# The head of an eight-core hybrid decoder step: x tiles 0 to 2 at once, v's weights in two halves, the other x tiles behind the first half

## The reference

```python
h = rmsnorm(x, g_mix)
proj = h @ w_in
a = proj[..., :512]
z = gelu(proj[..., 512:1536])          # u | v
u, v = z[..., :512], rmsnorm(z[..., 512:], g_v)
w = where(tril(ones(128, 128)), w_s, 0)
s = einsum('gij,bnjgc->bnigc', w, v in chunks of 128 rows) + b_s
pa = (trailing means of a over 2, 4, 8, 16 rows - a) @ w_pool * s_pool
merged = sigmoid(..) * (pa @ w_pool_out) + sigmoid(..) * ((u * s) @ w_gmlp_out)
x = x + merged @ w_out                 # then a SwiGLU FFN and a last rmsnorm
```

## Time and the profile before

| what | us |
|---|---|
| median of 3 runs | 832.25 |
| the profiled execution, its own time | 831.42 |
| span of its slowest core (core 2) | 829.6 |
| spans of the eight cores | 826.4 to 829.6 |
| PE busy on core 2 | 805.8 (97%) |
| DVE, ACT, POOL busy on core 2 | 380.8, 225.0, 96.2 |

### The profile page before, as it was taken

How to read it: one execution, slowest core, us unless ns; L and a number is a source line. 1 busy time by engine, 2 the same in 40 slices (tenths; PEclk the granted TensorE clock), 3 DMA queues, 4 the chain that set the end, 5 groups by cost and what they waited for, 6 DMA issues and landing times.

```text
span 829.6 us, 12893 instructions; the slowest of 8 cores (826.4 to 829.6 us)
## 1 busy us (share of the span) xinstructions
PE 805.8 (97%) x4423; PEld 425.6 (51%) x4474; DVE 380.8 (46%) x618; ACT 225.0 (27%) x458; POOL 96.2 (12%) x154
## 2 busy tenths in 40 slices
PE   5999999999999999999999999999999999999996
PEld 3465666645666666644444444444444444444442
DVE  3776444468222222265776935446711111115357
ACT  2654322224211211120136352322321111110023
POOL 2720000012000000000312000011200000000001
PEclk9999999999999999999999999999999999999998
DMA  7894155684974543354977417688576444336313
GB/s 167 182 181 84 26 77 77 102 122 86 198 114 69 80 74 66 63 92 65 144 238 112 77 28 135 112 170 136 95 117 102 77 77 77 66 62 102 51 48 155
DMA packets 57315, 85.14 MB, mean 103 GB/s; under 512 B 23373, under 2 KB 23749, under 8 KB 57236
## 3 DMA queue, kind: packets, MB, share of 16 engines
q0 software_dynamic: 30352, 57.97, 45.3%
q1 hardware_dynamic: 26755, 26.09, 11.3%
q10 hardware_dynamic: 146, 0.27, 0.1%
HBM read 128.72 MB, written 9.01 MB: 166 GB/s over the span
## 4 chain that ended last, share of the span: by engine, by line
PE 84%; DVE 6%; issue 3%; DMA 2%; POOL 2%; ACT 2%; DVEq 0%; SPq 0%; POOLq 0%; ACTq 0%
PE ps L347 81%; DMA xbuf<-xp 2%; POOL rs L384 1%; DVE xbuf L367 1%; ACT junk L375 1%; ACT junk L992 1%; DVE xbuf L984 1%; PE ps L746 1%; PE ps L742 1%; DVE ybuf L1017 1%; DVE hb L404 0%; POOL rs L1003 0%; PE ps L695 0%; DVE shr L627 0%; DVE xbuf L874 0%
## 5 line engine op out<-in xcount | busy, mean ns | idle before, releaser
L347 PE MATMUL ps<-hT,ring 128*128 128x384 bf16 (+2 forms) x2698 | 484.1, 337 | 1.2
L347 PEld LDWEIGHTS ps<-hT,ring 128*128 128x128 bf16 x2720 | 265.5, 98 | 206.3
L347 PE MATMUL ps<-ring,ovl 128*128 128x512 bf16 x939 | 207.3, 379 | 1.1
L846 DVE TENSOR_TENSOR ovl<-ftmp,ps 128x384 bf16<-128x384 f32 (+2 forms) x110 | 64.2, 584 | 233.8 <-PE ps L347 226.5
L347 PEld LDWEIGHTS ps<-ring,ovl 128*128 128x128 bf16 x960 | 93.5, 98 | 113.8 <-issue 2.2
L844 ACT ACTIVATE ftmp<-ps 128x384 f32<-128x384 f32 (+2 forms) x110 | 56.3, 515 | 232.0 <-PE ps L347 232.0
L267 POOL DMA_DIRECT2D ring<-wpk x60 | 45.0, 750 | 493.8 <-PE ps L347 459.9
L944 DVE TENSOR_TENSOR xbuf<-xbuf,ps 128x512 f32<-128x512 f32 x64 | 43.4, 687 | 41.2 <-PE ps L347 41.1
L347 PE MATMUL ps<-ovl,ring 128*128 128x384 bf16 (+2 forms) x317 | 62.0, 337 | 0.2
L812 DVE TENSOR_TENSOR shr<-shr,ps 128x384 f32<-128x384 f32 (+2 forms) x40 | 23.4, 585 | 83.3 <-PE ps L347 74.5
L992 ACT ACTIVATE junk<-xbuf 128x512 bf16<-128x512 f32 (+1 forms) x34 | 21.3, 627 | 124.0 <-DVE xbuf L984 120.9
(11 more groups left out here) (90 smaller groups left out, 346.8 us busy)
## 6 DMA issues: line engine op xcount, KB each, us to landing
ring<-wpk POOLq DMA_DIRECT2D x48, 1024.0 KB, 11.2
xbuf<-xp SPq DMA_DIRECT2D x16, 512.0 KB, 6.6
yp<-ybuf SPq DMA_DIRECT2D x11, 512.0 KB, 3.4
ring<-wpk POOLq DMA_DIRECT2D x8, 512.0 KB, 13.0
ring<-wpk POOLq DMA_DIRECT2D x4, 768.0 KB, 8.1
yp<-shr SPq DMA_DIRECT2D x4, 512.0 KB, 2.6
AB<-xp SPq DMA_DIRECT2D x2, 512.0 KB, 6.9
shr<-xp SPq DMA_DIRECT2D x2, 512.0 KB, 11.6
```

Of the source, the lines that this page charges most:

```text
L347: ins = e.matmul(out=out, lhsT=lhs_fn(i), rhs=rhs_fn(i), start=(i == 0), stop=(i == n - 1))
L846: P.op('dve', lambda e: e.tensor_tensor(out=actT[:, f, c0:c0 + W], in0=ftmp[:, fi, :W], in1=PS[bU][:, :W], op=ALU.mult), reads=[('ftmp', f ...
```

## The change

- SP issues x tiles 0, 8, 1 and 2 without a wait. Tiles 3 to 7 wait for the first half of v's weights.
- POOL issues v's weights (block 0) as two transfers of 128 x 2048, each with a semaphore of its own, and only once x tile 0 has landed.
- Blocks 0 and 1 are laid out in pieces of 2048 and 4096 elements a partition instead of 1024 (in both passes).
- v's 8 matmuls of a tile are issued as two parts of 4, one for each half of the weights; v runs one step of the stagger later. Gelu goes to `vg`, a float32 buffer with a place for each tile (it lies where `mergedT` will be), so nothing waits for `ftmp`. The squares of v and its 1/rms come later and in three batches of three tiles, one POOL pair for each batch, and `v_out` after each batch.
- The copies of `gv_rep` and `wb0` on DVE come later (at `i_ == 3`); blocks 1 and 2 are issued at `i_ == 7` and `i_ == 9` and the constants at `i_ == 8`.
- `ws_prep` comes after g = 2 instead of g = 0.

```diff
-WPIECE = 1024
+WPIECE = [2048 if i < 1 else 4096 if i < 2 else 1024 for i in range(len(WBLOCKS))]
...
+        def ring_issue_halves(j, after=()):
+            slot = j % NSLOT
+            off, ne = blocks[j]
+            for h_ in range(2):
+                dst = ring[:, slot, h_ * (ne // 2):(h_ + 1) * (ne // 2)]
+                src = wpk[0:1, off + h_ * 64 * ne:off + (h_ + 1) * 64 * ne].rearrange("o (p e) -> (o p) e", p=128)
+                P.dma('pool',
+                      (lambda e, dst=dst, src=src: e.dma_start(out=dst, in_=src)),
+                      'wh%d' % h_, reads=list(after), writes=[('ring', slot, h_)])
             rstate['issued'] = j + 1
...
-        for slot in range(2, 8):
-            xload(0, slot, after=[('x', 1, 0)])
+        xload(0, 2)
         cdma('pool', ident_b[:, :], c_ident[:, :], 'ident_b', own='c_idb')
-        ring_issue(0)
+        ring_issue_halves(0, after=[('x', 0, 0)])
+        for slot in range(3, 8):
+            xload(0, slot, after=[('ring', 0, 0)])
...
+                def v_mm(t_):
+                    if t_ == 0:
+                        v_part(0, 0)
+                    elif t_ == 1:
+                        v_part(1, 0)
+                        v_part(0, 1)
+                    elif t_ == 2:
+                        v_part(1, 1)
+                        v_part(2, 0)
+                        v_part(2, 1)
+                    else:
+                        v_part(t_, 0)
+                        v_part(t_, 1)
...
+                vsq_at = {9: (0, 1), 10: (2, 3), 11: (4, 5), 12: (6,), 13: (7,), 14: (8,)}
+                vrs_at = {11: 0, 12: 3, 14: 6}
                 warm(10)
-                for i_ in range(n_ + 8):
-                    at(i_ - 3, do_v)
+                for i_ in range(n_ + 6):
+                    at(i_ - 4, v_mm)
                     at(i_ - 1, lambda t_: hst[t_][2]())
                     at(i_ - 1, lambda t_: hst[t_][3]())
                     if i_ == 1:
                         warm(12)
+                    if i_ == 3:
+                        while row_later:
+                            row_later.pop(0)()
                     at(i_ - 2, lambda t_: hst[t_][4]())
-                    at(i_ - 7, lambda t_: vst[t_][2]())
                     at(i_, lambda t_: hst[t_][0]())
                     at(i_, lambda t_: hst[t_][1]())
-                    at(i_ - 6, lambda t_: vst[t_][0]())
-                    at(i_ - 6, lambda t_: vst[t_][1]())
-                    if i_ == 5:
+                    at(i_ - 5, v_gelu)
+                    for t_ in vsq_at.get(i_, ()):
+                        v_sq(t_)
+                    if i_ == 7:
+                        ring_issue(1)
+                    if i_ == 8:
                         late_pool_consts()
                         mid_sp_consts()
-                    if i_ == 8:
+                    if i_ == 9:
                         ring_issue(2)
+                    if i_ in vrs_at:
+                        lo_ = vrs_at[i_]
+                        v_rs(lo_, lo_ + 3)
+                        for t_ in range(lo_, lo_ + 3):
+                            v_out(t_)
...
-                if s == 0 and g == 0:
+                if s == 0 and g == 2:
                     ws_prep()
```

More of the change, by code:

```diff
@@ L549, in build_nc @@
                 hst = [norm_stages(slot, R, col0, gmix_rep, 'gmix', copy_eng='dve') for (slot, R, col0) in hts]
-                vst = {}
                 n_ = len(hts)
+                kv = [newcol() for _ in range(n_)]
                 def at(t_, fn_):
@@ L555, in at, with v_dst, v_part, fn @@
                         fn_(t_)
-                def do_v(t_):
-                    vst[t_] = c_tile(*hts[t_], split=True)
+                def v_dst(t_):
+                    slot, R, col0 = hts[t_]
+                    return vg[:, slot, :] if slot < 8 else ftmp[:R, 0, :]
+                vbank = {}
+                def v_part(t_, h_, wv=wv):
+                    slot, R, col0 = hts[t_]
+                    if h_ == 0:
+                        vbank[t_] = bank()
+                        held.add(vbank[t_])
+                    b = vbank[t_]
+                    def fn(e, wv=wv):
+                        ins = None
+                        for i in range(4 * h_, 4 * h_ + 4):
+                            ins = e.matmul(out=PS[b][:R, :], lhsT=hT[:, i, col0:col0 + R], rhs=wv[:, i, :],
+                                           start=(i == 0), stop=(i == 7))
+                        return ins
+                    P.op('pe', fn, reads=[cres_[h_]] + hT_res([slot]), writes=[('ps', b)])
@@ new lines, in v_mm, with v_gelu @@
+                def v_mm(t_):
[11 more added lines that the diff above has]
+                        v_part(t_, 1)
+                def v_gelu(t_):
+                    slot, R, col0 = hts[t_]
+                    b = vbank[t_]
+                    vd = v_dst(t_)
+                    P.op('act', lambda e: e.activation(out=vd, in_=PS[b][:R, :], func=AF.Gelu_apprx_tanh),
+                         writes=[('vg', slot), ('ps', b)] + ([('ftmp', 0)] if slot == 8 else []))
+                    held.discard(b)
@@ new lines, in v_sq, with v_rs @@
+                def v_sq(t_):
+                    slot, R, col0 = hts[t_]
+                    vd = v_dst(t_)
+                    k = kv[t_]
+                    ji = nxt('jk', 2)
+                    P.op('act', lambda e: e.activation(out=junk[:R, ji, 0:512], in_=vd, func=AF.Square,
+                                                       accum_out=ss[:R, k:k + 1]),
+                         reads=[('vg', slot)], writes=[('ss', k), ('junk', ji)])
+                def v_rs(lo, hi):
+                    ka, kb = kv[lo], kv[hi - 1] + 1
+                    P.op('pool', lambda e: e.tensor_scalar(out=ms[:, ka:kb], in0=ss[:, ka:kb], scalar1=1.0 / 512,
+                                                           scalar2=EPS, op0=ALU.mult, op1=ALU.add),
+                         reads=[('ss', k_) for k_ in range(ka, kb)], writes=[('ms', k_) for k_ in range(ka, kb)])
+                    P.op('pool', lambda e: e.tensor_tensor(out=rs[:, ka:kb], in0=ms[:, ka:kb],
+                                                           in1=mhalf[:, 0:1].to_broadcast([128, kb - ka]), op=ALU.pow),
+                         reads=[('ms', k_) for k_ in range(ka, kb)] + ['mhalf'],
+                         writes=[('rs', k_) for k_ in range(ka, kb)])
@@ new lines, in v_out @@
+                def v_out(t_):
+                    slot, R, col0 = hts[t_]
+                    vd = v_dst(t_)
+                    k = kv[t_]
+                    dst, dres = (vtok[:, slot, :], ('vtok', slot)) if slot < 8 else (vout[:, :], 'vout')
+                    P.op('dve', lambda e: e.scalar_tensor_tensor(
+                        out=dst, in0=vd, scalar=rs[:R, k:k + 1], in1=gv_rep[:R, :], op0=ALU.mult, op1=ALU.mult),
+                         reads=[('vg', slot), ('rs', k), 'gv'], writes=[dres] + ([('ftmp', 0)] if slot == 8 else []))
+                    if slot == 8:
+                        P.op('dve', lambda e: e.tensor_copy(out=vtok[:R, 8, :], in_=vout[:, :]),
+                             reads=['vout'], writes=[('vtok', 8)])
+                        P.dma('sp', lambda e: e.dma_start(out=nvs[:, :], in_=vout[:, :]), 'omisc', reads=['vout'])
@@ L823, in build_nc @@
                             out=mergedT[:, d, c0:c0 + W], in0=gab[:, gi, 0, :W], in1=gab[:, gi, 1, :W], op=ALU.add),
-                             reads=[('gab', gi, 0), ('gab', gi, 1)], writes=[('mergedT', d, c0)])
+                             reads=[('gab', gi, 0), ('gab', gi, 1)],
+                             writes=[('mergedT', d, c0)] + ([('vg', t_) for t_ in range(9)] if s == 0 else []))
                         if s > 0 and carry['late']:
```

32 lines of the change are left out of this document (19 added, 13 removed).

## The result

The changed kernel takes **838.7 us** (median of 4 runs, 836.77 to 838.96) beside 832.06 for the kernel before on the same chip: ratio 1.008, interval 1.0067 to 1.0093. It is slower by 0.8%, where 826.5 was forecast and 829.8 was the end of the range. The profiled execution took 836.77 us. Medians are of all executions; ratios, and what is said of compared runs, leave out those of the chip's slower state, in which the cores of a die ran much longer at a lower clock.

The account below looks back on a forecast made before the run. Start of projection a (A), set on core 2 by x's arrival, was taken to bound the kernel. Terms -4.15 (A) and -1.5 (after v) made -5.65 us: 831.42 to 825.8, median 826.6, stated 826.5; range 823.5 to 829.8.

Parts of the forecast that it names:

- block 1: Weight block needed at A: lands at 36.2, 1.6 us ahead; later block 2 and constants also cost nothing.
- A: Start of projection a on PE: forecast 37.85, 4.15 us less than 42.0, moving the end by as much.
- rival 2: Block 1 takes 14 us, lands at 40.2 and becomes the wait at A: 828.8 us, chance 0.10.
- rival 5: Slower: tiles 3 to 7 hang on a slow first half of v's weights, 834.2 us, chance 0.03.
- Block 1's issue: On POOL behind tile 6's 1/rms: tile lands near 23.8, 1/rms 2.37 us later, so issue at 26.2.
- H: Time the first half of v's weights has landed: taken as 12.5, bounds 10.6 and 14.
- from H to the landing of tile 3: Gated x load in the head: 4.9 us plus some 0.7 for the second half, 5.6 in all.
- from there to its transpose: Tile 3's landing to the end of `hb` in the head: 3.65 us, transpose beginning at 21.75.
- from there to A: PE work behind tile 3's transpose: 5 transposes and 7.5 tiles of v, 15.2 us, plus 0.9 for clock.
- The low clock: PE's slower matmuls after idling 2 to 3 us in the head: 0.9 us, bounds 0 and 1.75.
- the batches: After v, the trailing sums begin earlier against PE, removing waits: 1.5 us off, bounds 0 and 1.8.
- whatever the head did: The rest of the program from A to the end has the same length, 787.6 us, on both cores read.

Follow-up runs that it names:

- run 4: Kernel before the change, with only the changed order of issue (block 1 at i_ == 7, constants at 8, block 2 at 9): 838.69 us, ratio 1.0087.
- run 3: Changed kernel with block 1 issued at i_ == 5 instead of 7: 830.58 us, ratio 0.9992.
- run 15: Changed kernel with v's matmuls of tiles 0, 1, 8 and 2 ahead of tile 3's transposes, late issues kept: 836.77 us, ratio 1.0065.
- run 5: Changed kernel with block 1 at its old place and x tiles 3 to 7 gated on x tile 1: 830.18 us, ratio 0.9981.
- run 12: Changed kernel with v's matmuls of tiles 0, 1, 8, 2 ahead of tile 3's transposes, v one tile closer, block 1 at the fourth step: 829.52 us, ratio 0.9975.
- run 13: As run 12, with the seven constants issued without a gate: 826.93 us, ratio 0.9957.
- run 10: Kernel before with only v's batches, unscaled results, late mask and row copies; old loads and block 1 place: 831.10 us, ratio 1.0005.
- run 1: Changed kernel with the seven constants not waiting for block 1, issued behind x tile 7: 832.63 us, ratio 1.0021.
- run 2: Changed kernel with block 2 issued only after the v loop, ahead of block 3: 839.36 us, ratio 1.0094.
- run 11: Changed kernel with block 1 at its old place and in pieces of 1024 elements instead of 4096: 830.68 us, ratio 0.9999.
- run 7: Changed kernel's new loads alone, with the old v chain, order of copies and schedule: 832.06 us, ratio 1.0009.
- run 9: Changed kernel with block 1 at its old place and v's 12 remaining matmuls of tiles 0, 1, 8 ahead of tile 3's transposes: 829.34 us, ratio 0.9981.

## Why the prediction was wrong

**The step that failed** stands under block 1: "Block 2 and the constants come later still but have until A + 11 and more", costed at nothing. That edit of three moved calls decided the sign: run 4 makes it alone and loses 0.87%, 7.2 us; run 3 undoes one of them and wins 7.3 back. The time limit was if anything generous (on the good core 0 `sel` is used 54.70 - 38.53 = 16.2 us behind A, `ident_f` 17.5). What was missing is the other side of the comparison: the constants start when block 1 *lands*, 10 to 11 us behind its issue on the five late cores (8.1 to 8.4 on the three good ones); seven issues last another 6.5 us; and each then takes what it takes beside blocks 2 to 4, for `ident_f` 17.3 to 18.4 us on the late cores. Before, it was issued at 36.8 to 40.3 on all cores and took 9.8 to 12.5; on the late cores it is issued at 44.9 to 47.3. For `ident_f` on core 1 that is 29.8 + 11 + 6.5 + 17.7 = 65.0 us, against a use at A + 17.5 = 58.8. On the good core 0 it is 39.8 + 16.0 = 55.8 against 56.0: in time by 0.2. No rival had it either: rival 2 looked at block 1 itself, which landed 0.5 us before it was needed; rival 5 had the sign but another place.

**Block 1's issue** was put at 26.2, and came at 27.5 to 29.8. The sum let ACT square tile 6 when it lands; ACT does it in program order, on core 1 behind a gelu that waits for PE. That is a part only: with PE's new order it came 1.3 us earlier on average (run 15).

**The head.** The terms of the sum for A, forecast and measured (means of the eight cores, the range in brackets; H read from the issue of tile 3, which waits for it):

| term | forecast | measured |
|---|---|---|
| H | 12.5 | 14.1 (13.4 to 15.3) |
| from H to the landing of tile 3 | 5.6 | 5.4 |
| from there to its transpose | 3.65 | 3.8 |
| from there to A | 15.2 + 0.9 | 16.8 |
| A | 37.85 | 40.1 (38.5 to 41.3) |

H is the term that was too small by most, 1.6 us, and on two cores (14.7 and 15.3) well past its bound of 14. The rate of 2.2 us a tile held. The low clock cost the 12 matmuls behind the wait nothing on cores 0 and 6, where the wait was 1.58 and 0.85 us, and 1.0 to 2.5 us on the other six, behind waits of 2.51 to 4.55 (4.01 us against 2.85 on core 1, 5.31 on core 3), 1.5 on average: 0.9 was within the spread, the upper bound of 1.75 was not one. The Trainium skill, TensorE: Matmul & The Clock Gate, HAM oscillation, has PE start cold after each long enough wait, for which the prediction put 1.75; on those six cores the trace agrees, and they are nearer to that than to 0.9. No run shows a length of wait that decides it: core 0 of run 3 stayed at the higher level behind 3.52 us.

Under it lies one wrong idea, that order makes landings. Where the engines are busy at a share of 0.95 from 4 to 20 us, tile 3 lands when the bytes ahead of it are through, and run 5 shows that issuing it 5 to 6 us earlier is worth nothing. The forecast began at core 2 of the kernel before, whose engines stood idle for a moment at 16 us and had a share of 0.83 from 4 to 20; its gap was not that of the others, which had 0.91 to 1.05. The change put tile 2 and the weights ahead of tile 3; but PE's order made tile 3 the first thing that its queue had to have. That second half, the work that stands behind the wait and needs nothing new (12 matmuls, and 8 of tile 2), I had counted in the 15.2 us behind it as a given. Runs 12 and 13 move it ahead, and mean A falls by 2.0 and 2.4 us.

**What was right.** Where nothing is late behind A, the length behind it is one constant, and the batches shorten it: by 1.1 us (786.5 for 787.6, runs 3 and 10), where 1.5 was forecast and 0 to 1.8 given. The waits of 0.42 and 1.40 us are gone, one of 0.7 for DVE is left. But that the length is constant "whatever the head did" was read from two cores: core 3 of the kernel before has 789.2, since behind the same wait of 1.40 us its clock fell (0.52 granted from 63 to 66 us) and it took 2.64 us for 8 matmuls that take 1.46. The new gate and the halves cost nothing of themselves (run 5).

**The whole, by steps**, against the kernel before: forecast -5.7 us, measured +6.6 (838.7 - 832.06). Of the 12.3 between them the late issue is 7.3 (run 3 stands at -0.7 by its ratio), and the other 5.0 are the head's missing gain and 0.4 of the batches. PE's order and the constants' gate together give back 2.9 of them (run 13 stands at -3.6).

What stays open: why three of run 13's runs have a core or two at 829, since no profile caught one; what holds SP when it issues the constants on the late cores; what decides whether a wait brings the clock down; and what holds the engines at 212 to 222 GB/s while x and the weights are in flight together, where x alone reached 373.

## What to carry to other kernels

When an edit moves the *issue* of a transfer, follow everything that is gated on its landing to its own first use, and price each with the traffic that it will then share the engines with, not with its landing time in the old trace. Where the DMA engines are full, ask in what order bytes come through, not when they are issued, and put the work that needs no new data ahead of the wait on the in-order engine. And a wait has a second price, which can be larger than itself: behind 2.99 us of it TensorE took 2.77 us for what takes 1.46, behind 4.55 us it took 4.01 for 2.85, and on core 1 of run 1 a wait of 2.15 us was followed by some 5 us lost at the lower clock.

## What the runs showed of the hardware

- A constant of 60 KB took 3.9 to 5.6 us from issue to landing with block 2 out of its way (run 2, eight cores), and 11.1 to 16.3 beside such blocks (the changed kernel); 64 KB took 4.2 to 5.7 and 10.2 to 18.4.
- The length of one wait of PE doesn't tell whether the granted clock falls. It stayed at its higher level behind 1.58 us (core 0 of the changed kernel: 12 matmuls in 2.85 us), 2.90 (core 6 of run 11) and 3.52 (core 0 of run 3). It fell behind 1.40 us on one core of eight in the kernel before (core 3), behind 2.0 on five of eight in run 7, and behind 1.60 shortly after 1.92 in run 9.
- In two versions of one program the 512 KB x tile 3 landed at 20.9 us on the latest core whether it was issued at 8.1 or at 14.2, and at 19.5 and 19.6 on average.
